# Causal mask of the diagonal units: an affine selection by GpSimd on the probabilities, in place of a bf16 product over the scores on TensorE

## The reference, cut to what matters

```
proj  = x @ w_in                                  # all branch inputs in one projection
y_a   = gated DeltaNet, 4 heads of 128            # chunked, sequential over the sequence
y_b   = forgetting attention, 8 heads of 64:
        logits = q.k * d**-0.5 + cum[t] - cum[s]  # cum: cumulative sum of log_sigmoid(f + bias)
        logits = where(s <= t, logits, -inf)      # the causal mask
        o = softmax(logits) @ v
out   = LayerNorm(alpha * x + concat(y_a, y_b) @ w_out)
```

## Time and profile before

| | |
|---|---|
| median of three runs | 1553.09 us |
| profiled execution, its own time | 1557.39 us |
| its span, first to last instruction | 1555.3 us |
| mean granted TensorE clock | 0.982 of full speed |
| busy over the span: TensorE matmul | 1508.5 us (97%) |
| busy over the span: VectorE | 906.9 us (58%) |
| busy over the span: ScalarE | 615.2 us (40%) |
| busy over the span: GpSimd | 543.6 us (35%) |

### The profile page before, as it was taken

How to read it: one execution, slowest core, us unless ns; L and a number is a source line. 1 busy time by engine, 2 the same in 40 slices (tenths; PEclk the granted TensorE clock), 3 DMA queues, 4 the chain that set the end, 5 groups by cost and what they waited for, 6 DMA issues and landing times. The chain is left out here.

```text
span 1555.3 us, 21740 instructions
## 1 busy us (share of the span) xinstructions
PE 1508.5 (97%) x7720; PEld 1148.8 (74%) x7720; DVE 906.9 (58%) x1500; ACT 615.2 (40%) x1211; POOL 543.6 (35%) x454
## 2 busy tenths in 40 slices
PE   7999999999999999999998999999989999999998
PEld 5888888888888888888875666656656566577886
DVE  8455555555414766850215676777668687646755
ACT  1346354454611111113114556666555666621100
POOL 2212121121221111110103577677666767801111
PEclk9999999999999999999996899999999999999999
DMA  6134425262574343314547364665546465325632
GB/s 262 48 119 119 126 83 169 61 176 68 150 127 118 122 136 122 102 59 115 136 131 190 115 189 129 174 174 141 150 122 168 134 178 170 85 78 154 197 117 95
DMA packets 185792, 206.40 MB, mean 133 GB/s; under 512 B 45948, under 2 KB 129276, under 8 KB 182652
## 3 DMA queue, kind: packets, MB, share of 16 engines
q1 hardware_dynamic: 185108, 203.17, 45.7%
q10 hardware_dynamic: 576, 1.84, 0.3%
HBM read 129.79 MB, written 75.17 MB: 132 GB/s over the span
## 5 line engine op out<-in xcount | busy, mean ns | idle before, releaser
L554 PE MATMUL bank<-x_hi,w_hi 128*128 128x512 f32 x992 | 394.2, 397 | 0.0
L554 PE MATMUL bank<-x_hi,w_lo 128*128 128x512 f32 x992 | 387.1, 390 | 0.0
L554 PE MATMUL bank<-x_lo,w_hi 128*128 128x512 f32 x992 | 386.2, 389 | 0.0
L1575 POOL TENSOR_TENSOR m_acc<-m_acc,m_p 128x512 f32<-128x512 f32 (+1 forms) x252 | 299.9, 1190 | 75.9 <-ACT m_p L1544 51.3
L579 POOL TENSOR_TENSOR w_lo<-w_raw,w_hi 128x512 fp32r<-128x512 f32 x64 | 93.0, 1474 | 478.9 <-ACT w_hi L638 478.9
L1544 ACT ACTIVATE m_p<-m_st,fcol 128x512 f32<-128x512 f32 (+1 forms) x320 | 200.1, 637 | 131.8 <-PE m_st L1379 72.7
L554 PEld LDWEIGHTS bank<-x_hi,w_lo 128*128 128x128 f32 x992 | 186.1, 188 | 40.3
L554 PEld LDWEIGHTS bank<-x_lo,w_hi 128*128 128x128 f32 x992 | 186.6, 188 | 36.5
L554 PEld LDWEIGHTS bank<-x_hi,w_hi 128*128 128x128 f32 x992 | 186.4, 188 | 35.8
L1610 DVE TENSOR_REDUCE m_maxima<-m_aux 128x1 f32<-128x512 f32 x192 | 129.9, 685 | 74.7 <-PE m_aux L1341 68.9
L878 DVE SCALAR_TENSOR_TENSOR bank<-arena,taps,bank 128x512 f32<-128x512 f32 x144 | 108.8, 755 | 76.1 <-ACT bank L679 72.7
(11 more groups left out here) (211 smaller groups left out, 2403.6 us busy)
## 6 DMA issues: line engine op xcount, KB each, us to landing
w_raw<-in_w SPq DMA_DIRECT2D x31, 512.0 KB, 3.9
dram_feat<-ring SPq DMA_DIRECT2D x48, 256.0 KB, 4.2
arena<-dram_gates SPq DMA_DIRECT2D x32, 256.0 KB, 4.9
o_y<-dram_mixT SPq DMA_DIRECT2D x16, 512.0 KB, 6.2
o_x<-in_x SPq DMA_DIRECT2D x16, 512.0 KB, 4.1
out<-o_res SPq DMA_DIRECT2D x15, 512.0 KB, 5.0
arena<-in_xT SPq DMA_DIRECT2D x7, 1024.0 KB, 8.0
K<-dram_k_hi SPq DMA_DIRECT2D x12, 512.0 KB, 7.2
```

The lines of the kernel that those rows point to most:

```text
L554: mm = pe.matmul(banks[bank_of(s)][:], w[:, i % 2, k * P:(k + 1) * P], x[:, k, b * BLOCK:(b + 1) * BLOCK], start=(k == 0 and n == 0), stop ...
L1575: pool.tensor_tensor(total, total, p[u % PL][:, off:], ALU.add).then_inc(p_added, 1)
```

## The change

For a diagonal unit, the third product is gone and the scores are complete after the second. GpSimd, in slot s and ahead of the addition of unit s - 1, waits for the unit's exponential and overwrites the masked part of its probabilities in place: `affine_select` keeps an element where its column minus its partition (plus a base) is at least zero, and writes 0.0 elsewhere. It counts up the new semaphore `p_masked`. `values`, the addition of a diagonal unit, and the denominators of the very last group wait for it; `masked_through(s)` is the number of diagonal units up to s. The constants `over_k` and `ident_b` are still made.

```diff
+def masked_through(s):
+    return sum(UNITS[u][2] >= 4 * UNITS[u][1] for u in range(s + 1))
...
                         for u in direct:
-                            pe.wait_ge(p_ready, u + 1)
+                            pe.wait_ge(p_masked, masked_through(u))
...
-                    mm = pe.matmul(b[:, off:], K2[h % 2][:, keys], Q2[G % 4][:, off:], start=False, stop=not diagonal)
-                    if diagonal:
-                        mm = pe.matmul(b[:, off:off + cut.stop - cut.start], ident_b[:], over_k[:, cut],
-                                       start=False, stop=True)
+                    mm = pe.matmul(b[:, off:], K2[h % 2][:, keys], Q2[G % 4][:, off:], start=False, stop=True)
                     mm.then_inc(scores_ready, 1)
...
-                        pe.wait_ge(p_ready, s + 1)
+                        if diagonal:
+                            pe.wait_ge(p_masked, masked_through(s))
+                        else:
+                            pe.wait_ge(p_ready, s + 1)
                         pe.matmul(pv[half, off:], v[i % 2][:, kb, j, :], p[s % PL][:, off:], start=kb < 2,
                                   stop=kb >= 4 * g + 2).then_inc(pv_done, 1)
...
                 for s in range(END_SLOT + 1):
+                    if 0 <= s - 1 < N_UNITS and unit(s - 1)[4]:
+                        u = s - 1
+                        _, _, _, off, _, cut = unit(u)
+                        width = cut.stop - cut.start
+                        block = p[u % PL][:, off:off + width]
+                        pool.wait_ge(p_ready, u + 1)
+                        pool.affine_select(block, block, [[1, width]], ALU.is_ge, 0.0, base=P - width, channel_multiplier=-1)\
+                            .then_inc(p_masked, 1)
                     if 0 <= s - 1 < N_UNITS and UNITS[s - 1][2] > 0 and s - 1 <= last_unit(N_GROUPS - 1) - 4:
...
                         pool.wait_ge(p_ready, u + 1)
+                        if unit(u)[4]:
+                            pool.wait_ge(p_masked, masked_through(u))
```

More of the change, by code:

```diff
@@ L1151, in mix @@
         (v_landed, aux_ready, v_ready, mcol_ready, max_diag_ready, row_ready,
-         scores_ready, p_ready, p_added, pv_done, odd_ready, both_ready, gated_ready, yb_ready) = (sem(n) for n in (
+         scores_ready, p_ready, p_added, p_masked, pv_done, odd_ready, both_ready, gated_ready, yb_ready) = (sem(n) for n in (
              "v_landed", "aux_ready", "v_ready", "mcol_ready", "max_diag_ready", "row_ready",
-             "scores_ready", "p_ready", "p_added", "pv_done", "odd_ready", "both_ready", "gated_ready", "yb_ready"))
+             "scores_ready", "p_ready", "p_added", "p_masked", "pv_done", "odd_ready", "both_ready", "gated_ready", "yb_ready"))
         norm_landed, half_w_ready, S_zeroed, XT_zeroed = (sem(n) for n in (
```

## The result

The changed kernel takes 1570.54 us (median of 4 runs, 1567.97 to 1571.69) against 1553.05 beside it: a ratio of 1.0106 (95% interval 1.0085 to 1.0128), 17.5 us slower. Forecast were 1577, in a range of 1556 to 1616. The two profiled executions differ by 14.6 us in span (1569.9 against 1555.3), all of it in `mix`; the mean granted clock of these two is 0.981 against 0.982. The profiled execution of before is 4.3 us above its median, which is why the two differences aren't the same.

What follows compares the result with a forecast made beforehand. TensorE's own stream was taken to bound `mix`. Stalls 38.5 plus score banks 2.2 less products 15.4 gave 25.3 us; less 2.8 of denominator waits, plus 1.7 for the clock: 1553.1 + 24 = 1577 us, range 1556 to 1616.

Steps and rivals of the forecast that it cites:

- Direction and mechanism: In `mix`, TensorE's values stall behind GpSimd's queue for the selections, outweighing the removed products; slower had 0.85.
- The selection's price: On GpSimd, each added selection takes 0.40 us for 128 columns and 0.60 for 256.
- The stalls: TensorE waits in `values` for GpSimd's selections in 23 of 32 groups, 38.5 us in all.
- the ledger: TensorE's and GpSimd's queues carried through all 32 groups of `mix`: 25.3 us longer, 15.6 with cheaper selections.
- three worked examples: Ends of groups 3, 26 and 13 in `mix`: stalls of 3.9 us, 3.9 us and none.
- The score banks' 2.2 us: The score banks in `mix` add 2.2 us to the stalls in the values.
- The product's 15.4 us: On TensorE in `mix`, removing 128 products at 0.12 us each saves 15.4 us (5 to 29).
- The clock: After long TensorE stalls in `mix`, one drop to 1.2 GHz for most of 4 us costs 1.7 us.
- rival 4: Seven long TensorE stalls each bring a clock drop, 12 us by price: 1587; counted within the forecast's 0.64.
- GpSimd's slack: GpSimd's waits for exponentials in `mix`, 95.5 us before, were to fall below 40 us.
- Rival 1: GpSimd becomes the bound of `mix`, from 0.61 us a selection: 1606 or 1633; chance 0.21.
- Rival 2: Selections stay hidden on GpSimd, in time for TensorE, which keeps the 15.4 us: 1538 or 1548; chance 0.07.

Runs made afterwards that it cites:

- the pair with both moves: GpSimd's power and the values each one slot later: kernel before with these 1551.99 us, and the same without product or selection 1544.99 us.

## Why the prediction was right, step by step
- **Direction and mechanism** were right. The slowdown is TensorE standing in the values behind GpSimd's queue; nearly all of it goes when GpSimd's standing is moved or the values come later, grows with a dose of selections, and stays when the product is put back.
- **The selection's price** was put at 0.40 and 0.60 us and is 0.33 and 0.40. The rows had it: the copy's 0.292 us was the nearest row, and the memset's 0.85 ns a column gives the 256 columns. From 128 to 256 columns a selection takes 0.11 us more (0.293 in the median against 0.398). The Trainium skill's faster figure (GPSIMD Engine Reference, section Performance pitfalls for Q7 kernels) is 1.03 cycles an element; at the 1.2 GHz of that page it gives an estimate of 0.11 us for these 128 columns, which the trace bears out, and its 2.03 cycles an estimate of 0.22, which it doesn't.
- **The stalls** were 38.5 us in the sum and are 22.5 by the starts (27.9 on the loads). Of the miss of 16 us the price above is about half: the ledger had 38.5 for 59 us of selections and 28.8 (its 15.6 us, less 2.2, plus 15.4) for the faster ones of some 42 us, which puts the measured 45 us at about 31, an estimate. For the rest, no run shows which of the ledger's delays was too long. Of the three worked examples group 3 lost 3.4 us and group 26 lost 2.5, where 3.9 were forecast for each, and group 13 nothing. 12 groups stalled and not 23, and the groups of 16 units have 13.5 of the 22.5 us, again the largest share. (The two masked times in the examples should be 908.0 and 1282.1, 0.1 us earlier.)
- **The score banks' 2.2 us.** The loads of the scores wait 9.3 us for exponentials (7.0 before), but also 8.8 in the run without product and selection. Little of it can come from the selections.
- **The product's 15.4 us** is the other mis-sized term of the sum, beside the stalls. It was read from starts on TensorE, and these do move by 0.12 to 0.13 each. But I took TensorE for the only bound, because a matmul was under way for 96% of the block. With the product gone the kernel gains 1 to 2 us in the medians, 7 in the pair with both moves; at the same clock it is 4.6 and 6.3. The rest turns into waits, of which those for exponentials and sums show. That the total still came out near is luck in part: a gain too large by 9 to 10 us stood against stalls too large by 16. With the measured terms the sum closes: 22.5 - 2.8 - 5 = 14.7 us, and the two profiled executions differ by 14.6.
- **The clock.** I counted one more drop to 1.2 GHz, 1.7 us. The two profiled executions have the same clock within 0.001, but that of before is one of its slower ones. The four executions of the changed kernel have 0.9825 in the mean, 76 of before in the other sets 0.986. At 1.2 us for each 0.001 that is about 4 us of the 17.5, more than my 1.7 and less than rival 4's 12. It is an estimate and not shown: the changed kernel with the product kept had 0.9854, as before. Group 3's stalls brought no drop here, and did where the selections were doubled and where TensorE stood for the denominators instead (above). The Trainium skill (TensorE: Matmul & The Clock Gate, section What's actually happening) says that the array falls to 1.2 GHz after an idle stretch; the two drops, each behind a stretch with long waits, agree.
- **GpSimd's slack** was to fall below 40 us and is 68.8, since the selections took 45 us and not 59, and since TensorE's stalls make the block longer and give GpSimd time. Rival 1, GpSimd as the bound, is out even for the doubled selections (453 of 573 us busy, and it still waits for exponentials). Rival 2 was right on what it needs, GpSimd being in time; with the two moves it comes true, at 5 us below before and not at 15.

What stays open is how the 0.12 us of a product become 0.05, spread over waits of a few tenths each; no run takes the exponentials' waits away alone. Open too is whether the changed kernel's lower clock comes from its stalls; no run holds the clock fixed.

## What to carry to other kernels
Before giving an engine a new task, look at where in its queue the task will stand and what that queue waits for, not at its busy share: here 35% busy over the span (70% in this block) hid waits of 46 us for a third engine, behind which every new dependency had to queue. When a change moves a producer later, move its consumer or whatever blocks the producer's queue as well, and time the two moves in the old kernel too. A start-to-start distance on a nearly full engine can be more than its removal is worth; here it was more than twice that. Before you explain a few microseconds between two kernels, set their granted clocks side by side.

## What the runs showed of the hardware
An affine selection of 128x128 f32 in place on GpSimd takes 0.29 us in the median (0.33 in the mean, 0.75 at most), of 128x256 0.40: as much as a copy. A bf16 product of 128 columns between fp32 ones costs 0.12 to 0.13 us of start-to-start distance on TensorE, three times the 0.04 from its own start to the next. Behind a stretch in which TensorE had matmuls under way for 1.83 of 4 us, and behind one of 1.45 of 4, the granted clock was 0.50 and 0.55; behind one of 3.34 of 5 us it was 1.00.
